# Two products of layer 2 made side by side, and copied out unscaled by ScalarE

## The reference, cut to what matters

```
n = rms_norm(h, mix_norm_g)
z = n @ w_in
a, gate, c_q, c_kv, k_r = split(z, ...)
u = a * sigmoid(gate)
u = causal_depthwise_conv(u, conv_w, conv_b)      # 31 taps
...
q  = rms_norm(c_q, q_norm_g) @ w_uq
kv = rms_norm(c_kv, kv_norm_g) @ w_ukv
... attention over q, kv, rope(k_r); then both halves are normed and multiplied by w_out
```

## Time and profile before

| | |
|---|---|
| median of 3 runs | 4046.9 us (4045.6 to 4049.49) |
| profiled execution: time, span | 4044.52 us, 4042.7 us |
| mean granted clock of PE | 0.94 |
| PE busy | 3695.7 us, 91% |
| DVE busy | 1740.0 us, 43% |
| ACT busy | 1099.2 us, 27% |
| POOL busy | 1068.7 us, 26% |

### The profile page before, as it was taken

The page is one execution under the profiler, slowest core; times in us unless marked ns, Lnnn a source line. Parts: engine busy times, 40 slices in busy tenths (PEclk is TensorE's granted clock), DMA queues, the critical chain, the costliest instruction groups (busy, mean ns, idle before and its releaser), DMA issues.

```text
span 4042.7 us, 40236 instructions
## 1 busy us (share of the span) xinstructions
PE 3695.7 (91%) x16870; PEld 2930.3 (72%) x16870; DVE 1740.0 (43%) x1763; ACT 1099.2 (27%) x1381; POOL 1068.7 (26%) x1136
## 2 busy tenths in 40 slices
PE   8888698999999789999999999999979899999797
PEld 6555376888887488665568899989857777777576
DVE  3444544222222668455336555445463322344313
ACT  3333234111111522222333111111142432322232
POOL 3111143222233233000002344334322222211053
PEclk9898899999999889999799999999989999999699
DMA  3000031111111111000011111111121111000133
GB/s 111 21 21 21 16 115 58 48 49 49 47 47 48 63 58 42 11 6 6 6 53 37 42 48 48 47 48 47 42 84 37 52 58 47 27 30 23 48 121 108
DMA packets 55900, 191.23 MB, mean 47 GB/s; under 512 B 6804, under 2 KB 7188, under 8 KB 55208
## 3 DMA queue, kind: packets, MB, share of 16 engines
q1 hardware_dynamic: 55720, 188.66, 13.5%
HBM read 171.78 MB, written 16.86 MB: 47 GB/s over the span
## 4 chain that ended last, share of the span: by engine, by line
PE 83%; DVE 10%; ACT 5%; issue 1%; DMA 1%; SPq 0%; DVEq 0%; ACTq 0%
PE psum L263 21%; PE psum L265 21%; PE psum L264 21%; PE psum L136 18%; DVE res L96 2%; DVE work L96 1%; DVE res L105 1%; DVE mix L105 1%; ACT work L124 1%; ACT L124 1%; DVE work L114 1%; ACT res L124 1%; ACT w_hi L129 1%; DVE x_lo L96 1%; PE psum L296 1%
## 5 line engine op out<-in xcount | busy, mean ns | idle before, releaser
L96 POOL TENSOR_TENSOR w_lo<-w_raw,w_hi 128x256 fp32r<-128x256 f32 x1132 | 1068.5, 975 | 2939.1 <-ACT w_hi L129 2939.1
L263 PE MATMUL psum<-x_hi,w_hi 128*128 128x512 f32 (+2 forms) x3472 | 1315.7, 379 | 82.7 <-DVE x_lo L96 30.7
L264 PE MATMUL psum<-x_lo,w_hi 128*128 128x512 f32 (+2 forms) x3472 | 1265.1, 364 | 0.0
L265 PE MATMUL psum<-x_hi,w_lo 128*128 128x512 f32 (+2 forms) x3472 | 1262.1, 364 | 0.0
L263 PEld LDWEIGHTS psum<-x_hi,w_hi 128*128 128x128 f32 x3472 | 664.6, 191 | 206.7 <-issue 66.7
L129 ACT CAST w_hi<-w_raw 128x1024 fp32r<-128x1024 f32 x283 | 296.6, 1049 | 1723.8 <-PE psum L265 1706.7
L264 PEld LDWEIGHTS psum<-x_lo,w_hi 128*128 128x128 f32 x3472 | 664.9, 192 | 98.0 <-issue 20.5
L265 PEld LDWEIGHTS psum<-x_hi,w_lo 128*128 128x128 f32 x3472 | 662.1, 191 | 85.7
L263 PE MATMUL psum<-h_hi,w_hi 128*128 128x512 f32 x864 | 346.0, 400 | 31.6 <-issue 10.3
L265 PE MATMUL psum<-h_hi,w_lo 128*128 128x512 f32 x864 | 343.6, 398 | 0.0
L264 PE MATMUL psum<-h_lo,w_hi 128*128 128x512 f32 x864 | 341.3, 395 | 0.0
(11 more groups left out here) (250 smaller groups left out, 3511.9 us busy)
## 6 DMA issues: line engine op xcount, KB each, us to landing
w_raw<-w_dram SPq DMA_DIRECT2D x283, 512.0 KB, 3.2
res<-spill SPq DMA_DIRECT2D x4, 1044.0 KB, 9.4
res<-x_dram SPq DMA_DIRECT2D x8, 512.0 KB, 9.7
res<-x_dram SPq DMA_DIRECT2D x4, 1024.0 KB, 8.0
spill<-res SPq DMA_DIRECT2D x1, 4096.0 KB, 12.1
spill_a<-mix SPq DMA_DIRECT2D x8, 512.0 KB, 2.6
res<-spill_a SPq DMA_DIRECT2D x4, 1024.0 KB, 8.2
x_plain<-spill SPq DMA_DIRECT2D x4, 1024.0 KB, 10.1
```

Of the source, the lines that this page charges most:

```text
L96: self.mark(self.e.tensor_tensor(out, a, b, op), inc)
L263: t.e.matmul(out, whi, xhi, start=k == 0, stop=False, skip_group_check=True)
L264: t.e.matmul(out, whi, xlo, start=False, stop=False, skip_group_check=True)
L265: ins = t.e.matmul(out, wlo, xhi, start=False, stop=last_k, skip_group_check=True)
```

## The change

`pe_first` takes the place of the first call of `pe_gate`. It claims both slots, makes the first third of gate 0 and then of a 0, and then goes through the operand rows of the second half: for each, the second and the last third of gate 0, and the same of a 0. The ones product comes behind both. ACT, in `act_gate` for c = 0, copies both products out of PSUM as they are, gate 0 into `sig` and a 0 into `u_pad`, before it makes the root's first value. DVE multiplies `sig` and later `u_pad` in SBUF, in place. A semaphore `gate_scaled` tells ACT that `sig` is scaled; `rope`, weights and transfers are issued as before. The other three gate pairs are unchanged.

```diff
 def pe_gate(self, t, c):
     self.pe_in(t, ("gate", c), 512 + c * P)
-    if c == 0:
-        self.pe_ones(t, ("rms",), self.total, self.ffn.x2_total, 14, self.rms_sum)
     self.pe_in(t, ("a", c), c * P)
+
+def pe_first(self, t):
+    k, x2_ready, products = self.k, self.ffn.x2_ready, []
+    for name, col in (("gate", 512), ("a", 0)):
+        tile, at = divmod(len(k.blocks), BLOCKS)
+        assert at == 0
+        k.blocks += [block_of("w_in_2", c, col) for c in range(8)]
+        p, before = k.claim((name, 0), 3, 348)
+        for stream, value in before:
+            t.wait_ge(stream, value)
+        products.append((p, tile))
+
+    def step(p, tile, i, c):
+        t.wait_ge(k.w_ready, 4 * tile + c // 2 + 1)
+        t0, m = THREE[i]
+        w = k.w_hi[tile % 3][:, c, :], k.w_lo[tile % 3][:, c, :]
+        return k.three(t, k.ps[:, p.first + i, 0:m], w, (k.hi(c)[:, t0:t0 + m], k.lo(c)[:, t0:t0 + m]), c == 0, c == 7)
+
+    for p, tile in products:
+        for c in range(8):
+            t.wait_ge(x2_ready, c + 1)
+            step(p, tile, 0, c)
+    for c in range(8):
+        t.wait_ge(x2_ready, 8 + c + 1)
+        for p, tile in products:
+            step(p, tile, 1, c)
+            ins = step(p, tile, 2, c)
+            if c == 7:
+                k.close(t, ins, p, True)
+    self.pe_ones(t, ("rms",), self.total, self.ffn.x2_total, 14, self.rms_sum)
...
-        for c in range(2):
-            self.pe_gate(t, c)
+        self.pe_first(t)
+        k.label(("a", 0))
+        self.pe_gate(t, 1)
...
         if c == 0:
+            for name, out in (("gate", self.sig), ("a", self.u_pad[:, 0, CONV2 - 1:])):
+                p = self.k.products[name, 0]
+                a.wait_ge(*p.done)
+                a.copy(thirds_of(out), self.k.view(p), inc=p)
             self.act_root(a, ("rms",), self.rms, 1, D)
-        a.wait_ge(*p.freed)
+            a.wait_ge(self.gate_scaled, 1)
+        else:
+            a.wait_ge(*p.freed)
         a.act(self.sig, self.sig, ACT.Sigmoid, inc=self.gate_sig)
...
         if c == 0:
             self.dve_root(v, ("rms",), self.rms, self.M[2], 1, D)
-        v.settle()
-        v.tt(thirds_of(self.sig), k.view(p), thirds_of(self.rms), ALU.mult, inc=p)
+            v.wait_ge(*p.freed)
+            v.tt(self.sig, self.sig, self.rms, ALU.mult, inc=self.gate_scaled)
...
+        if c == 0:
+            v.wait_ge(*p.freed)
+            v.tt(u, u, self.sig, ALU.mult)
```

More of the change, by code:

```diff
@@ L1213, in __init__ @@
         self.rope_landed, self.rms_sum, self.rms_guess = s("rope_landed"), s("rms_sum"), s("rms_guess")
-        self.gate_sig = s("gate_sigmoid")
+        self.gate_sig, self.gate_scaled = s("gate_sigmoid"), s("gate_scaled")
         self.row_square, self.row_total = s("latent_square"), s("latent_total")
@@ L1749, in dve_gate @@
         p = k.products["gate", c]
-        v.wait_ge(*p.done)
         if c == 0:
             self.dve_root(v, ("rms",), self.rms, self.M[2], 1, D)
-        v.settle()
-        v.tt(thirds_of(self.sig), k.view(p), thirds_of(self.rms), ALU.mult, inc=p)
+            v.wait_ge(*p.freed)
+            v.tt(self.sig, self.sig, self.rms, ALU.mult, inc=self.gate_scaled)
+        else:
+            v.wait_ge(*p.done)
+            v.settle()
+            v.tt(thirds_of(self.sig), k.view(p), thirds_of(self.rms), ALU.mult, inc=p)
         advance(branch, self.TAPS["gate"][c][0])
@@ L1759, in dve_gate @@
         v.settle()
-        p = k.products["a", c]
-        v.wait_ge(*p.done)
-        v.tt(thirds_of(self.u_pad[:, c, CONV2 - 1:]), k.view(p), thirds_of(self.sig), ALU.mult, inc=p)
+        p, u = k.products["a", c], self.u_pad[:, c, CONV2 - 1:]
+        if c == 0:
+            v.wait_ge(*p.freed)
+            v.tt(u, u, self.sig, ALU.mult)
+        else:
+            v.wait_ge(*p.done)
+            v.tt(thirds_of(u), k.view(p), thirds_of(self.sig), ALU.mult, inc=p)
     def dve_row(self, v, i, n):
```

## The result

| | before | after |
|---|---|---|
| median of 4 runs | 4046.25 us (4042.4 to 4049.49) | 4025.97 us (4017.24 to 4029.57) |
| ratio, 95% interval | | 0.9947 [0.9927, 0.9967] |
| profiled execution: span | 4042.7 us | 4027.8 us |

The change won 20.3 us in the medians. The forecast was 18.5 us and 4028.4 us. Of all executions reported in this text two were far slower than the rest, both of e7 (4460.39 us at a granted clock of 0.779, and 14026.04 us), and its median and ratio leave them out.

What follows compares the result with a forecast made beforehand. TensorE was taken as the bound (busy 91% of the span, 83% of the chain). First tap 14.9 + DVE's waits 6.3 - slow clock 2.7 = 18.5 us off a median of 4046.9 gave 4028.4 us, range 4022 to 4037.

Steps and rivals of the forecast that it cites:

- The bound and the mutual wait: Layer 1 to 2: TensorE bounds; PE waits 10.18 us for gate 0's banks, then DVE 12.27 us for a 0.
- PE in the loop: Norm's x_lo rows: 12 matmuls per row, 1.9 us within 2.02, at 2.4 GHz; a 0 ends at 1425.5.
- slow loop: Rival: PE at 1.2 GHz in the x_lo loop; 8 us won (chance 0.05), or 16.9 if the clock rises (0.10).
- the rule that spoke against the forecast: Skill page on cycling through PSUM banks with small idles: by it PE would be slow throughout the new x_lo loop.
- ACT: Before the root: two added copies of 1.05 us each; Ln starts at 1429.15 instead of 1431.82, 2.66 us earlier.
- First tap: Start of the convolution on DVE: at 1442.3 instead of 1457.19, 14.9 us earlier.
- Where the stall goes: Up to c 0: DVE loses 6.3 us of waits; c 0 about 21.2 us earlier, behind a PE wait of 7.4 us.
- The clock behind that wait: At c 0: PE starts at 1.2 GHz, 21 slow matmuls, price 2.7 us, bounds 0 and 9.4.
- The sum: Whole kernel: 14.9 + 6.3 - 2.7 = 18.5 us won, to 4028.4 us.
- The rest moves as one block: Behind c 2: both queues stand to each other as before, so everything later shifts together.
- an attention that takes longer: Layer 2: an attention longer than now was named as a sign that the prediction is wrong.
- slower: Rival, layer 2's attention: shifted start brings 48 us more of lower-clock stretches, costing 24, total 4052; chance 0.04.

Runs made afterwards that it cites:

- e7: The change with ScalarE's weight cast moved behind the root's first value and five taps moved behind the rotated key row; median 4021.38 us, ratio to before 0.9945.
- e1: Against the kernel before: only gate 0 copied out by ScalarE, products in the old order, a 0 multiplied out of PSUM; 4033.97 us, ratio 0.9969.
- e2: The change with both products still made side by side, but only gate 0 copied; a 0 stays in PSUM for VectorE; 4034.65 us, ratio to before 0.9975.
- e6: The change with ScalarE's weight cast moved from ahead of the two copies to behind the root's first value; 4021.83 us, ratio to before 0.9946.
- e3: The change with five taps moved from ahead of the rotated key row to behind it; 4017.71 us, ratio to before 0.9934.
- e5: The change with its second loop turned: all of gate 0's 48 matmuls, then all of a 0's, not row by row; 4026.09 us, ratio to before 0.9960.
- e9: The change with ScalarE's order gate 0's copy, weight cast, root's first value, a 0's copy; 4022.59 us, ratio to before 0.9948.
- e10: The same kernel as e3 (the change, five taps behind the rotated key row), run again beside the change; 4021.90 us, ratio to before 0.9941.
- e11: The same kernel as e7 (the change, cast behind the root, five taps behind the rotated row), run again; 4022.68 us, ratio to before 0.9944.

## Why the prediction was right, point by point

**The bound and the mutual wait.** Right. e1 shows the half of it (freeing gate 0's banks removes the wait, 10.1 us of the stage), e2 the other (a 0's banks must come free too).

**PE in the loop.** Right: 2.4 GHz throughout, a 0's last matmul ends 1427.31 + 0.32 - 1424.37 = 3.3 us behind the row; forecast 1425.5 - 1422.26 = 3.2. The rival "slow loop", and with it the rule that spoke against the forecast, didn't come: PEclk is 1.00 in the loop, with banks that change after each triple. (By its own factors the rival's 27.9 us are 96 x 0.29 = 27.8; nothing follows from it.)

**ACT.** Right: copies of 1.02 and 1.03 us against 1.05. Ln came 1430.98 - 1424.37 = 6.61 us behind the row, forecast 1429.15 - 1422.26 = 6.9.

**First tap.** 34.93 - 20.12 = 14.8 us earlier; forecast 14.9. One small term was missed: the last multiplication took 1.67 us instead of 1.25. It now reads two operands from SBUF while POOL rounds (from 1442.56, shown under e6); in e1 and e2, where it reads a 0 out of PSUM beside the same rounding, it took 1.25. The 0.42 us were made up, by luck, by the root's being 0.3 us earlier than worked out.

**Where the stall goes.** Right in place and size: no wait of DVE for PE up to the rotated row, its banks free 94.67 - 73.34 = 21.3 us earlier (forecast 21.2), and PE waits 7.13 us before c 0 (forecast 7.4). e3 confirms the cause: with five taps less ahead of the rotated row the wait shrinks from 7.13 to 2.21 us.

**The clock behind that wait.** Right in kind, too big in size. It fell, but for 10 matmuls, not 21. From the free banks to the end of the stage the change takes 165.37 - 73.34 = 92.0 us and before took 184.98 - 94.67 = 90.3: a price of 1.7 us in place of 2.7. e5 paid with 15 slow matmuls at the same place.

**The sum.** 14.8 + 6.5 - 1.7 = 19.6 us in the stage, against 18.5.

**"The rest moves as one block."** This is the step that didn't hold to the last us. From the eighth x_lo row to the start of the attention's second head the change is 278.67 - 258.43 = 20.2 us shorter. The third head then takes 3.2 us more, in each of its three profiles; the prediction had named an attention that takes longer as a sign of being wrong, and up to this size it came. From the fourth head to the end before takes 4042.7 - 1912.7 = 2130.0 us, the change 2130.1 in one profile and 2116.3 in the two others. And ahead of all this, in layer 1, whose code is untouched, the change's profiles are 2.0 to 2.3 us later than before's at the eighth x_lo row. So 20.2 - 3.2 - 2.1 = 14.9 us is the difference of the two spans shown above, and 28.5 to 28.9 that of the others.

Over all its 14 executions the change has a median of 4021.9 us (4015.6 to 4030.2); before has medians of 4044.0 to 4045.8 on the three chips of the experiments, so some 23 us were won. The forecast of 18.5 lies between the 14.9 and the 28.9 us of single profiles. What was right by its mechanism is the stage and what follows up to the second head. That the median of the result came within 2.4 us of the forecast is in part luck: -2.1, -3.2 and 0 to +13.8 us, none of them in the sum, happened to come to little.

The windows put 7.8 of the 13.8 us on PE's clock; for the rest, in layer 3, a window with a higher granted clock was read but not the whole sum. Why the better course became more frequent when the stretch began some 17 us earlier stays open; I didn't test it. What makes layer 1 later stays open too, but the rows place it near the start: DVE's rows of the change and of before are level within 0.1 us at 101 us and 2.1 us apart at 229, with PEclk 0.82 and 0.86 from 101 to 131 us, and e1 and e9, with the same code there, are 0.3 us earlier than before at the eighth x_lo row. In the prediction the attention's clock was the place of the rival "slower"; in the third head it went that way by 3.2 us, and behind the fourth head's start it went the other way in two of the three profiles.

No version that I tried beats the change by more than the runs scatter: e3, e9, e10 and e11 have shorter stages by 0.5 to 3.2 us, medians of 4017.7 to 4022.7 us, and reach the piece of 156 matmuls within 0.2 us of the change.

## What to carry to other kernels

When two engines wait for each other through one buffer, copy the operand out raw and put the scale on later: two copies of 1.0 us here freed 27 us of TensorE's queue and 19.6 us of the stage, while the first copy gave 10.1 us of the stage in the old order and 10.2 in the new one. Then follow both queues to the next place where they meet; the gain is what the slower queue moves, 21 us at the rotated row here, not what the freed engine could. And before moving a short instruction off the path, look at what its consumer does on another engine, for that moves with it.

## What the runs showed of the hardware

A wait of 2.21 us before c 0 was followed by a fall of PE's clock to 1.2 GHz in e1, e3, e10 and e11, for 12 matmuls and beginning about 1 us behind the restart. The same wait left it at 2.4 GHz in both profiles of before, in e2 and in e9. I had taken 2.21 us to be safe.

Behind longer waits (7.1 us in the change and e5, 4.7 in e9, 13.1 in e2, 10.2 in before) the matmuls that ran slow were 10, 15, 16, 19 and 21, of 0.13 us extra each: a price of 1.3 to 2.7 us that isn't ordered by the length of the wait.

In layer 2's attention the granted clock is at 0.50 for stretches in which PE is busy all the time, and 156 matmuls of one piece took 41.8 or 49.6 us in two executions of one kernel.

A DVE tensor_tensor of 128x1044 with both inputs in SBUF took 1.67 us in place of 1.25 beside POOL's rounding, and the tensor_scalar 1.24 in place of 0.70 (e6). The multiplication of a 0 took 1.67 us with both inputs in SBUF (the change, e9) and 1.25 with one of them in PSUM (e1, e2), each time beside a rounding.
